# A mixture-of-experts stage: experts taken in an order ranked by count, 20 positions with 96 places and 12 with 64, and w1 in four loads of 2 MB

## The reference

```
    logits = (xt @ w_router).astype(jnp.float32) + b_router.astype(jnp.float32)
    top_val, top_idx = lax.top_k(logits, TOP_K)
    gates = jax.nn.softmax(top_val, axis=-1)
...
        hid = x_pad[toks] @ w1[e] + b1[e]
        glu = jnp.minimum(hid[..., :D_FF], SWIGLU_LIMIT)
        lin = jnp.clip(hid[..., D_FF:], -SWIGLU_LIMIT, SWIGLU_LIMIT)
        act = glu * jax.nn.sigmoid(SWIGLU_ALPHA * glu) * (lin + 1)
        return (act @ w2[e] + b2[e]).astype(jnp.float32) * wts[:, None]
```

## Time and profile before

| | us |
|---|---|
| median of 3 runs | 1778.97 (1778.77 to 1779.12) |
| the profiled execution, its own time | 1777.86 |
| its span, first to last instruction | 1776.2 |
| mean granted TensorE clock | 0.993 |

### The profile page before, as it was taken

One profiled execution on the slowest core, in us unless ns is written; L12 is line 12 of the kernel. 1 busy time (PEld: TensorE's weight loads), 2 busy tenths in 40 slices (PEclk: granted clock), 3 DMA queues, 4 the chain that ended last, 5 costly groups with the idle time before them and its releaser, 6 DMA issues.

```text
span 1776.2 us, 36374 instructions
## 1 busy us (share of the span) xinstructions
PE 1735.3 (98%) x15357; PEld 839.6 (47%) x15357; DVE 638.4 (36%) x1067; ACT 222.9 (13%) x466; POOL 288.9 (16%) x364
## 2 busy tenths in 40 slices
PE   7999999999999999899999999999999999999996
PEld 5666675554554445433443434344343444434344
DVE  4554546444451014641221313223131322313236
ACT  2312221221220101100000100000010000000001
POOL 2010011000005001412122121212212121221201
PEclk9999999999999999899999999999999999999999
DMA  6332332111115224299999999999999999999995
GB/s 198 122 106 61 118 121 61 56 39 50 35 35 165 78 86 174 101 415 415 418 418 417 420 418 420 419 418 420 417 420 417 420 419 418 420 418 421 418 419 220
DMA packets 133664, 489.91 MB, mean 276 GB/s; under 512 B 17376, under 2 KB 70956, under 8 KB 84416
## 3 DMA queue, kind: packets, MB, share of 16 engines
q1 hardware_dynamic: 118672, 458.30, 64.9%
q0 software_dynamic: 13584, 30.49, 4.9%
q10 hardware_dynamic: 1360, 0.45, 0.1%
HBM read 472.27 MB, written 25.07 MB: 280 GB/s over the span
## 4 chain that ended last, share of the span: by engine, by line
PE 93%; DVE 3%; DMA 3%; issue 0%; ACT 0%; POOL 0%; SPq 0%; ACTq 0%; POOLq 0%; DVEq 0%
PE PS L1861 36%; PE PS L409 21%; PE PS L1873 17%; PE PS L1686 6%; PE PS L1774 3%; PE PS L1648 2%; PE PS L1729 2%; DMA ring<-y_dram 1%; PE PS L1600 1%; DMA ring<-in_w 1%; PE PS L1733 1%; PE PS L1719 1%; DVE x_sb L1468 1%; PE PS L1537 1%; DMA x_sb<-in_x 0%
## 5 line engine op out<-in xcount | busy, mean ns | idle before, releaser
L1861 PE MATMUL PS<-ring,mix_sb 128*32 128x512 f32 x6144 | 668.8, 595 | 1.4 <-DVE mix_sb L1394 1.0
L1861 PEld LDWEIGHTS PS<-ring,mix_sb 128*32 128x32 f32 x6144 | 204.5, 110 | 446.7 <-issue 435.0
L1873 PE MATMUL PS<-ring,hm_sb 128*32 128x256 f32 x6144 | 337.5, 379 | 0.0
L1873 PEld LDWEIGHTS PS<-ring,hm_sb 128*32 128x32 f32 x6144 | 204.2, 110 | 140.6 <-issue 18.7
L1437 DVE TENSOR_TENSOR low_sb<-PS,low_sb 128x1536 f32<-128x1536 f32 x32 | 56.2, 1758 | 591.6 <-PE PS L1861 591.6
L409 PE MATMUL PS<-uT_sb,ring 128*128 128x512 f32 (+3 forms) x400 | 141.9, 511 | 0.0
L952 ACT ACTIVATE hm_sb<-hm_sb 128x768 f32<-128x768 f32 x32 | 27.0, 844 | 709.3 <-DVE hm_sb L1439 709.3
L756 POOL COPY ints<-ints 128x3 int32 (+1 forms) x30 | 5.6, 187 | 667.1 <-ACT hm_sb L958 667.1
L705 POOL DMA_INDIRECT mix_sb<-xt_dram,ints x96 | 98.9, 1030 | 56.7 <-POOL ints L745 24.0
L409 PEld LDWEIGHTS PS<-uT_sb,ring 128*128 128x128 f32 x400 | 75.4, 190 | 64.3 <-issue 59.3
L731 POOL DMA_INDIRECT y_dram<-hm_sb,ints x90 | 90.9, 1009 | 47.2 <-POOL ints L756 25.5
(11 more groups left out here) (301 smaller groups left out, 1299.0 us busy)
## 6 DMA issues: line engine op xcount, KB each, us to landing
ring<-in_w SPq DMA_DIRECT2D x384, 1024.0 KB, 16.6
ring<-in_w_in SPq DMA_DIRECT2D x24, 512.0 KB, 4.0
ring<-in_w_in SPq DMA_DIRECT2D x8, 1024.0 KB, 5.3
y_dram<-at_sb POOLq DMA_DIRECT2D x4, 2048.0 KB, 10.6
ring<-y_dram SPq DMA_DIRECT2D x4, 2048.0 KB, 20.9
ring<-m_dram POOLq DMA_DIRECT2D x16, 256.0 KB, 4.9
ring<-in_w_m_proj SPq DMA_DIRECT2D x8, 512.0 KB, 4.2
ring<-in_w_a_proj SPq DMA_DIRECT2D x8, 512.0 KB, 4.1
```

The lines of the kernel that those rows point to most:

```text
L1861: last = nc.tensor.matmul(PS[32 * j:32 * j + 32, at + t, :].rearrange("p (c n) -> p c n", c=2), xgT[n][:, k, 32 * t:32 * t + 32], w1_c[k][ ...
L1873: last = nc.tensor.matmul(PS[32 * j:32 * j + 32, Y_BANK + t, 0:QR], actT[:, k, 32 * t:32 * t + 32], w2_in[k // 2][:, k % 2, j * QR:(j + 1) ...
```

## The change

1. **Order by count.** TensorE counts each expert's tokens (as before), DVE ranks the experts by count on the chip (`key_row`, `above`, `rank_col`), and a permutation matrix `perm_e` turns position into expert. Expert 0 keeps position 0. SP reads the expert's number for each position from a table in SBUF (`ids_i`, `expert_of`).
2. **Places by position.** The positions have 3, 3, 2 groups of places in turn, ten times, and 2, 2 at the end (`GROUPS`): 20 positions with 96 places and 12 with 64. The experts with the smallest counts get the short ones. Up, down, DVE, ACT, gathers and scatters take only the groups of the position.
3. **The table** now lies with the expert as the slowest dimension. It comes in as one load with the expert on the partition, and 24 small products with `perm_e` put its columns in the order of the positions.
4. **Loads.** w1 comes in four loads of 2 MB (two pieces each); w2 stays at four of 1 MB. w2 of expert 0 is loaded right behind the projection.
5. **Loops** have six experts in their body.
6. Half of the output bias products stand inside up of expert 0. The overflow sums take the 64 places into account and run to up to 24 turns.

The core of the diff:

```
+GROUPS = [3, 3, 2] * 10 + [2, 2]
+FULL = GROUPS.count(3)
+PERIOD = 6
+LAST_P = (E - 2) // PERIOD
...
+def groups_at(i, r):
+
+    return GROUPS[i * PERIOD + r] if isinstance(i, int) else GROUPS[r % PERIOD]
...
-        def load_w1(k, e):
-            sp.dma_start(w1_c[k].rearrange("p c n -> p (c n)"),
-                         w1v[:, bass.ds(e, 1), k, :].rearrange("p e n -> p (e n)")).then_inc(chunk_in[k], 16)
+        def load_w1(c, e):
+            sp.dma_start(w1_pair[c], w1v[:, bass.ds(e, 1), 2 * c:2 * c + 2, :].rearrange("p e k n -> p (e k n)")).then_inc(chunk_in[2 * c], 16)
...
+            for c in range(4):
+                if c < 3:
+                    sp.wait_ge(w1_used, i * (KT - 1) + (2 * c + 3 - KT))
...
+        st.did(V.scalar_tensor_tensor(key_row, PS[:, 6, 2 * E:3 * E], 32.0, ct[:, K_KEY:K_KEY + E], ALU.mult, ALU.add))
+        st.did(V.scalar_tensor_tensor(key_col, PS[:, 6, 3 * E:3 * E + 1], 32.0, ct[:, K_KCOL:K_KCOL + 1], ALU.mult, ALU.add))
...
+        st.alone(V.tensor_scalar(above, key_row, key_col, None, ALU.is_gt))
+        st.alone(V.tensor_reduce(rank_col, above, AX.X, ALU.add))
+        dve.wait_ge(pos_used, TOTALS_READ)
+        V.tensor_scalar(perm_e, ct[:, K_RNK:K_RNK + E], rank_col, None, ALU.is_equal).then_inc(pos_used, 1)
...
+        st.alone(V.tensor_tensor(above_all, key_row.unsqueeze(1).broadcast_to([P, E, E]), key_row.unsqueeze(2).broadcast_to([P, E, E]), ALU.is_gt))
+        st.alone(V.tensor_reduce(short, above_all, AX.X, ALU.add))
...
-            for t in range(TT):
+        def up(e, n, k, g, at=0):
+            if k % 2 == 0:
+                pe.wait_ge(chunk_in[k], e * 16 + 16)
+            for t in range(g):
```

More of the change, by code:

```diff
@@ L70, in constant_tables @@
     c[0:96, K_SEL:K_SEL + E] = np.arange(96)[:, None] % 32 == np.arange(E)
+    c[:, K_KEY:K_KEY + E] = -np.arange(E)
+    c[:, K_KCOL] = -(np.arange(P) % E)
+    c[:, K_KEY] = 1e6
+    c[::E, K_KCOL] = 1e6
+    full = np.array(GROUPS) == 3
+    c[:, K_RNK:K_RNK + E] = np.where(full, np.cumsum(full) - 1, FULL + np.cumsum(~full) - 1)
+    c[:, K_ROW:K_ROW + E] = (np.arange(P) % E)[:, None]
     half = ROPE // 2
@@ L398, in build @@
     done = [planes[m][:, 0, :] for m in range(MT)]
+    w1_pair = [view(ring, slot(CHUNK_SLOT[2 * c]), 2 * SLOT) for c in range(4)]
     w2_c = [view(ring, slot(CHUNK_SLOT[8 + c]), 2, D) for c in range(4)]
@@ L536, in load_down @@
                 load_w2(c, e)
-        for k in range(KT):
-            load_w1(k, 0)
+        for c in range(4):
+            load_w1(c, 0)
         def store_xt(m):
@@ L702, in gather @@
         def gather(n, idx):
-            for t in range(TT):
+            for t in range(len(idx)):
                 pool.indirect_dma_start(out=xg[n][:, t, :], out_offset=None, in_=xt_dram,
@@ L1841, in _ @@
         pe.wait_ge(pos_used, MT)
-        group(pe, PS[:, 6, 2 * E:3 * E], [(ones, sel[:, n, :]) for n in range(MT)]).then_inc(pe_pos, 1)
+        group(pe, PS[:, 6, 2 * E:3 * E], [(ones, sel[:, n, :]) for n in range(MT)])
+        for j in range(4):
+            totals = group(pe, PS[E * j:E * j + E, 6, 3 * E:3 * E + 2], [(sel[:, n, :], ones[:, 0:2]) for n in range(MT)])
+        totals.then_inc(pe_pos, 1)
         turn_gates(last)
@@ L1869, in down @@
                 if k % 2 == 0:
-                    pe.wait_ge(chunk_in[at + k // 2], e * 16 + (16 - 16 * elsewhere))
-                for t in range(TT):
+                    pe.wait_ge(chunk_in[sems[k // 2]], e * 16 + 16 if landed is None else landed)
+                for t in range(g):
                     for j in range(4):
@@ L1898, in _ @@
         for k in range(KT):
-            up(0, 0, k, Y_BANK)
-        pe.wait_ge(sum_added, 2 * MT)
-        step(1, 1, False)
-        step(2, 0)
-        with nc.Fori(1, E // 2 - 1, engines=[pe.engine], head_slot={pe.engine: 0}) as i:
-            step(i * 2 + 1, 1)
-            step(i * 2 + 2, 0)
-        step(E - 1, 1)
+            up(0, 0, k, TT, Y_BANK)
+            if k == 0:
+                pe.wait_ge(pos_used, IDS_KNOWN)
+                bias2(0)
+            if k == 2:
+                pe.wait_ge(sum_added, 2 * MT)
+                pe.wait_ge(tab_in, 16)
+                for j in range(4):
+                    for t in range(TT):
+                        for v in range(2):
+                            row = nc.tensor.matmul(PS[32 * j:32 * j + 32, 3, (2 * t + v) * E:(2 * t + v + 1) * E], tab_e[0:E, t, :, v], perm_e[0:E, :], start=True, stop=True)
+                row.then_inc(pe_pos, 1)
+        step(0, 1, False)
+        for r in range(2, PERIOD):
+            step(0, r)
+        with nc.Fori(1, LAST_P, engines=[pe.engine], head_slot={pe.engine: 0}) as i:
+            for r in range(PERIOD):
+                step(i, r)
+        step(0, E - 2)
+        step(0, E - 1)
         def rows_of(m, n):
-            for t in range(TT):
+            for t in range(GROUPS[E - 2 + n]):
                 for j in range(4):
```

295 lines of the change are left out of this document (169 added, 126 removed).

## The result

The changed kernel is slower, by a little: 1782.89 us (median of 19 runs) against 1778.97 for the kernel before (19 runs), a ratio of 1.0022 with a 95% interval of 1.0015 to 1.0028, so +3.9 us. Forecast were 1769 us and a range of 1756 to 1780. The time lies outside the range, on the side to which the prediction gave a chance of 0.12.

What follows compares the result with a forecast made beforehand. It took the transfers, at 31.5 us an expert, to bound the kernel once TensorE's work shrinks. Start -6, w1 in 2 MB -6.6 and loops +3 summed to -9.6 us from 1778.97: 1769 us, range 1756 to 1780.

Steps and rivals of the forecast that it cites:

- What bounds it: Expert stage: transfers need 31.5 us an expert; with short positions TensorE averages 27.3 and waits 4.2 us an expert.
- TensorE as the only bound: Rival for the expert stage: shorter up and down save 124 us, time near 1665; chance 0.02.
- Loops of six experts: TensorE's larger loop body: 75 code fetches of 16 KB, spread over 16 DMA engines, +3 us, bounds 0 and +47.
- The stall at the entries: TensorE's loop entries: 4 us at each of four, falling in its wait of 4.2 us an expert.
- Start: Start of the transfer stream: w2 of expert 0 loaded early, up(1) at 767.6; -6 us, bounds -8 and -1.
- w1 in 2 MB: w1 loads: 16 KB packets save 0.23 us an expert over 29 experts; -6.6 us, bounds -9 and -1.
- Tail: After the last plane lands: same planes and order, still 20.1 us, so zero change.
- three signs of being wrong: TensorE still without gaps, stage GB/s below 415, or up(1) starting after 773.
- the last plane at 1746: End of the transfer stream: expected sign that the last plane lands near 1746.
- slower by code: Rival for the loops: all 75 refetches on one DMA engine add 47 us, time 1813; chance 0.08.

Runs made afterwards that it cites:

- e1: Changed kernel with positions ordered as 20 of 96 places, then 12 of 64, so every loop body holds two experts; 1770.92 us, ratio 0.9957 to the kernel before.
- e3: Changed kernel with TensorE's loop of six experts written out, so no back edge but as much code to fetch; 1780.60 us, ratio 1.0007.
- e5: Kernel of e1 with TensorE's loop over positions 2 to 19 written out; 1777.65 us, ratio 0.9997.
- e4: Changed kernel with the second bias product behind w1's second piece and the overflow sums behind the transposition of expert 1; 1778.98 us, ratio 1.0010.
- e7: Kernel of e1 with the two start moves of e4 added; 1763.91 us, ratio 0.9922.
- e2: Changed kernel with each w1 pair loaded as two 1 MB transfers in 8 KB packets on one semaphore; 1792.74 us, ratio 1.0079.
- e8: Kernel of e7 with the 12 short positions spread, mostly one short and one long expert per TensorE body; 1764.79 us, ratio 0.9928.
- e6: The kernel before, with only w1 changed to four loads of 2 MB; 1773.95 us, ratio 0.9977.
- e10: Kernel of e8 with w2 too in loads of 2 MB; 1759.60 us, ratio 0.9893.

## Why the prediction was wrong

In the terms of its sum, by the profiled executions (span 1776.2 to 1779.5, +3.3 us, where -9.6 was forecast):

- **What bounds it: right.** The transfers are the limit, TensorE waits 68 us in all on the ring at 92% busy, the packets are of 16 KB, the queue counts agree. TensorE as the only bound (1665) is out.
- **Loops of six experts, +3: the step that failed.** It cost 11 to 12 us. e1 has its last plane at 1751.4, the changed kernel at 1761.0. Taking out its start, which was 1.1 us worse (399.66 MB to go at 800 us without code, against 399.19), the body of six costs 10.8 us; by the medians 12. I had the count right: 75 fetches forecast, 74 between 900 and 1700. I had the mechanism too, and the wrong price. A fetch moves 16 KB as a packet of weights does, so I gave it 0.63 us; the share of 0.6% (rounded) of 16 engines over 800 us is 77 us for 74, 1.04 us each, and the landings of the last engine move by 1.5. The packets' own times in the trace have a mean of 1.07 us for a fetch and 0.62 us for a 16 KB packet of w1. And I spread them evenly. Spread evenly, 1.04 us on one of 16 engines is 0.065 us a fetch; e3 and e5 measured 0.148 and 0.145. So the engine that counts bears more than its even share: over twice at 1.04 us a fetch, and by the steps counted at e5, one fetch in eight, just twice. The cost lies within the bounds of 0 to +47 that I gave the term, but the forecast was added up with 3. The earlier trace rows already held the first error: 0.7% of 16 engines over 135 us is 15 us for 14 packets, 1.08 each.
- **The stall at the entries, nothing: nearly.** I let it fall in TensorE's wait. My 4 us were 2.47 of standstill and 1.7 of a slower up behind it; the three back edges stood still for 6.1, 5.5 and 5.5 us, and the ups behind them took 23.4, 22.2 and 22.4 us where 20.8 is the full clock, so 7 to 9 us each. In e3 their absence is worth at most 2 to 3 us of the time in all. The Trainium skill (Runtime: NRT & Kernel Launch, Instruction fetch mechanics) calls crossing a 16 KB boundary of straight code mostly hidden. For TensorE it is (e3 shows no gap there), for the DMA engines it is not: the 7 us from e1 to e5 are such fetches. Its warning about taken branches agrees with the three standstills.
- **Start, -6: measured -0.8.** up(1) began at 770.4 and not 767.6, the first pair came free at 750.9 and not 748.2. Two parts are known: the overflow sums ended at 768.4 and not 766 (e4), and the first piece of up(0) took 4.69 us at half clock, where I had put 2.6. I priced the small operations well (table products 1.41 us against 1.2), and had the 1.7 us that a slower clock cost up(0) before only as a possibility for the last pair, not in the first piece. e7 shows that 5 us more were to be had there.
- **w1 in 2 MB, -6.6: right in kind and about right in size.** Last planes of e1 and before, less the start (0.15 MB, +0.4 us): -5.1 us, part of it held back by TensorE until 1400. Taken away from the changed kernel (e2) it is 9.9, beyond my bound of 9. The 6 ns that I found in each packet were too few; what a larger packet saves beyond them no run tells.
- **Tail, 0: -1.6.** Small, and no run looks into it.

-0.8, -5.1, +10.8 and -1.6 give the +3.3. Of the 12.9 us between it and the forecast of -9.6, the loops are 7.8 and the start 5.2; either one right would have brought the time back into the range. None of my three signs of being wrong came (TensorE has gaps, GB/s is 419, up(1) started at 770.4): GB/s is a sum over 16 engines, and the loads wait for one of them. What did not come is the last plane at 1746. The rival that went this way was slower by code, with all refetches on one engine (1813); I said that it decides from 13 us, and it came to 11 to 12. I had held it off with the landing time that fell after the first pass. That was a median over loads, in a stretch of 100 us in which the queue may have had time to empty (not shown): it could not show what one engine got.

## What to carry to other kernels

Where transfers set the pace of a stage, a loop body whose code is fetched again in every pass is paid for in DMA time, even when the engine that runs it has waits to spare: look at the instruction queue of the stage, and keep the body small by an order of the shapes that repeats soon (sorted as in e1, or by turns as in e8). Price a fetch by its own row in the profile and by the engine that gets most of them, since each load waits for its last engine. When two limits are level, lifting one alone gives only the distance to the other: packets alone gave 3 to 4 us (e6), packets and short positions with small loop bodies gave 7.5 (e1), 13 with the start mended (e7) and 19 with the packets of w2 as well (e10).

## What the runs showed of the hardware

- An instruction fetch of 16 KB keeps a DMA engine for 1.04 us by the queue's share, where a data packet of the same size takes 0.63 us. The last landing of a load moves by some 1.5 us about once in eight fetches (8 steps for 64 in the changed kernel, 7 for 59 in e3, 5 for 40 in e5). That each step is one fetch on the engine that lands last is the reading that fits, but it is not shown: the trace does not name the engine of a fetch. Why a step is longer than a fetch, and why the last engine gets twice an even share, is open.
- After 6.1 us without a product TensorE came back at 1.2 GHz (granted clock 0.50) for 5 us; after two gaps of 5.5 us the mean granted clock of the next 5 us was 0.66 and 0.64, and the up there took 1.4 and 1.7 us longer.
- Runs of 16 KB in place of 8 KB raised the whole stage from 414 to 419 GB/s (w1, e2 to the changed kernel), and from 423 to 425 (w2, e8 to e10).
- A loop body of TensorE of some 1,552 instructions ran without a fetch from 895 to 1700 us (the kernel before); one of some 4,150 was fetched in every pass, 74 packets of 16 KB from 900 to 1700 us.
